# A mixture-of-experts kernel: later slot weights, a weight place used once, and a hint ahead of a jump

## The reference, cut to what matters

```python
def hier_moe(h, w_group, b_group, w_expert, b_expert, w1, w3, w2):
    gl = (hf @ w_group) + b_group                 # 4 groups: the best one by argmax
    g_w = softmax(gl)[g_idx]
    el = (hf @ w_expert)[group g_idx] + b_expert  # 8 experts in it: the best two
    vals, idx = top_k(softmax(el), 2)
    weights = g_w * vals / sum(vals)
    # each of 32 experts works on the rows routed to it:
    y = (silu(x @ w1[e]) * (x @ w3[e])) @ w2[e]   # 1024 -> 512 -> 1024, float32
    # and its rows, times their weights, are added to their tokens
```

## Time and profile before

| | |
|---|---|
| median of 3 runs | 1852.88 us |
| profiled execution | 1853.75 us, span 1851.7 us |
| TensorE busy | 1764.1 us, 95% |
| VectorE / ScalarE / GpSimd busy | 48% / 33% / 7% |
| DMA | 333.57 MB, 180 GB/s over the span |
| mean granted TensorE clock | 0.984 of full |

### The profile page before, as it was taken

The page is one execution under the profiler, slowest core; times in us unless marked ns, Lnnn a source line. Parts: engine busy times, 40 slices in busy tenths (PEclk is TensorE's granted clock), DMA queues, the critical chain, the costliest instruction groups (busy, mean ns, idle before and its releaser), DMA issues.

```text
span 1851.7 us, 25714 instructions
## 1 busy us (share of the span) xinstructions
PE 1764.1 (95%) x10733; PEld 1333.8 (72%) x10733; DVE 893.7 (48%) x1841; ACT 619.6 (33%) x1080; POOL 136.8 (7%) x96
## 2 busy tenths in 40 slices
PE   6999999997999999999989999998999899999998
PEld 5878766886655555555569967666788798888886
DVE  4355454454355555645553577655734532222223
ACT  3434454422111111111242456554524432222222
POOL 1000110221000000000001000011101000000221
PEclk9999999998999999999999999998999999999999
DMA  6512100358899999999955221013420232223201
GB/s 251 191 46 81 57 23 24 131 195 332 330 406 416 402 401 399 400 416 413 429 214 186 91 106 67 1 46 123 162 92 12 91 103 91 93 90 137 91 23 46
DMA packets 76449, 333.57 MB, mean 180 GB/s; under 512 B 6407, under 2 KB 14215, under 8 KB 63400
## 3 DMA queue, kind: packets, MB, share of 16 engines
q1 hardware_dynamic: 72472, 325.04, 45.4%
q0 software_dynamic: 2560, 4.20, 0.7%
q10 hardware_dynamic: 1296, 2.62, 0.4%
HBM read 325.55 MB, written 10.49 MB: 181 GB/s over the span
## 4 chain that ended last, share of the span: by engine, by line
PE 82%; DMA 7%; DVE 5%; ACT 3%; issue 2%; POOL 0%; SPq 0%; DVEq 0%; ACTq 0%; POOLq 0%
PE ps L558 78%; DMA arenaf<-in_w 2%; DMA splitf<-in_w 2%; DMA hf<-in_w 2%; PE ps L977 1%; PE ps L2975 1%; PE ps L2113 1%; DVE arenaf L3057 1%; PE ps L812 1%; DVE splitr L623 0%; ACT splitr L634 0%; DVE arenaf L3075 0%; ACT arenaf L966 0%; DVE hr L866 0%; DVE xf L3353 0%
## 5 line engine op out<-in xcount | busy, mean ns | idle before, releaser
L558 PE MATMUL ps<-hr,splitr 128*128 128x512 f32 (+1 forms) x2784 | 576.2, 367 | 6.7 <-POOL hr L909 4.3
L558 PEld LDWEIGHTS ps<-hr,splitr 128*128 128x128 f32 x2784 | 474.9, 192 | 87.7 <-issue 4.9
L558 PE MATMUL ps<-splitr,hr 128*128 128x512 f32 (+1 forms) x1488 | 273.8, 344 | 2.2 <-DVE hr L1074 1.4
L558 PEld LDWEIGHTS ps<-splitr,hr 128*128 128x128 f32 x1488 | 234.3, 190 | 35.8 <-issue 2.0
L623 DVE TENSOR_TENSOR splitr<-ring,splitr 128x2048 fp32r<-128x2048 f32 x61 | 142.8, 2343 | 230.6 <-ACT splitr L634 230.5
L2233 DVE TENSOR_TENSOR xf<-xf,ps 128x512 f32<-128x512 f32 x248 | 153.5, 682 | 70.8 <-PE ps L558 70.6
L634 ACT CAST splitr<-ring 128x2048 fp32r<-128x2048 f32 x61 | 116.1, 1905 | 143.9 <-PE ps L558 142.8
L2187 ACT ACTIVATE junkr<-ps,arenaf 64x512 fp32r<-64x512 f32 x62 | 42.3, 682 | 296.6 <-PE ps L558 295.9
L623 DVE TENSOR_TENSOR splitr<-arenaf,splitr 128x2048 fp32r<-128x2048 f32 x27 | 63.3, 2345 | 104.9 <-ACT splitr L634 104.9
L558 PE MATMUL ps<-arenaf 128*64 128x128 f32 (+7 forms) x784 | 103.1, 342 | 5.5 <-ACT arenaf L984 3.5
L558 PE MATMUL ps<-splitr,otr 128*128 128x512 f32 x384 | 88.6, 391 | 1.2 <-DVE arenaf L3828 1.2
(11 more groups left out here) (408 smaller groups left out, 1983.0 us busy)
## 6 DMA issues: line engine op xcount, KB each, us to landing
ring<-in_w SPq DMA_DIRECT2D x22, 2048.0 KB, 31.6
arenaf<-in_w SPq DMA_DIRECT2D x22, 2048.0 KB, 31.6
splitf<-in_w SPq DMA_DIRECT2D x21, 2048.0 KB, 34.7
hf<-in_w SPq DMA_DIRECT2D x20, 2048.0 KB, 32.0
ring<-in_w_in SPq DMA_DIRECT2D x11, 2048.0 KB, 12.0
otf<-in_w SPq DMA_DIRECT2D x11, 2048.0 KB, 32.0
ring<-in_w_gate_up SPq DMA_DIRECT2D x7, 2048.0 KB, 7.8
arenaf<-in_w_in SPq DMA_DIRECT2D x4, 2048.0 KB, 8.8
```

The lines of the kernel that those rows point to most:

```text
L558: return te.matmul(out, lhsT, rhs, start=start, stop=stop)
```

## The change

Four things are changed.

1. The products that make the slot weights leave `pe_router` and become `pe_slot_weights`, called for expert 0 behind both up products and the second expert's first transposes. VectorE's two steps behind them move in the same way (`ve_slot_weights`).
2. A tenth place is added (`carve(7168, KC)`, in the arena where the router's tables lie). It holds one entry only, the 26th (w3 of expert 3): no entry follows it there. All later entries move to other places, and the first three loads behind the experts are tied to uses one entry later. SyncE loads it in `sp_router`, when the first gather, the slot roots and OW8 are done.
3. To make room, the tables that are still read then (O8, rk8, tokens, cnt) move to the arena's end, and B8, OW8 and R8 into `junk`. The overflow tables, computed in the same room, wait for the tenth place to be used, so VectorE's pieces begin at expert 4, with two pieces at experts 4 and 5.
4. TensorE's branch past the overflow code is written out as `br_cond` with a `BRANCH_PREFETCH_HINT` that stands ahead of the down product of expert 29.

```diff
         SLOT = [ring0[:, 0:KC], ring0[:, KC:2 * KC], arena[:, 0:KC], OT[:, 0:KC], Hf[:, KC:2 * KC],
-                Sf[:, 0:KC], Sf[:, KC:2 * KC], Hf[:, 0:KC], carve(3072, KC)]
+                Sf[:, 0:KC], Sf[:, KC:2 * KC], Hf[:, 0:KC], carve(3072, KC), carve(7168, KC)]
...
-        extra_places = (3, 8, 5 + wo_end[0] % 2, 7, 5 + wo_end[1] % 2, 4)
+        once = 9
+        extra_places = (3, 8, 5 + wo_end[0] % 2, 7, 5 + wo_end[1] % 2, 4, once)
...
-            if n < len(entries) and not (n >= moe_end and experts_alone):
+            if n < len(entries) and place[c] != once and not (n >= moe_end and experts_alone):
...
-        O8, e8, rk8, q8 = v3(32, 8), v3(1, 8), v3(1, 8), v3(32, 8)
+        O8, rk8 = thirds(carve(11312, 256), 8), thirds(carve(11864, 8), 8)
+        e8, q8 = v3(1, 8), v3(32, 8)
...
-        B8, OW8 = thirds(carve_r(10800, 256), 8), thirds(carve(11056, 256), 8)
+        B8, OW8 = thirds(junk_r[:, 0:256], 8), thirds(junk[:, 256:512], 8)
...
+            def pe_slot_weights():
                 ps = take("slot weights")
...
                 vstep(ve.tensor_tensor(OW8, O8, W8.broadcast_to([128, 8, 32]), ALU.mult), ("slot weights",))
+            def ve_slot_weights():
                 for w in ve_at(("weight sum",)):
...
                 sp_load(more_first + 5)
+                for w in sp_at(("rows", 0), ("root sum",), ("slot weights",)):
+                    sp.wait_ge(*w)
+                sp_load(more_first + 6)
...
                     if b == 0:
                         pe_first_rows(1)
+                        pe_slot_weights()
                     if b < 31 and b % 2:
                         pe_rows((b + 1) // 2)
+                    if b == 30 and live:
+                        branch_ahead.append(te.mark_branch_hint_location())
                     if b:
                         pe_down(b - 1)
...
-                    if 2 <= b < 22:
-                        go(places_, 1)
+                    if 4 <= b < 22:
+                        go(places_, 2 if b < 6 else 1)
...
             def ve_extra_places():
+                for w in ve_at(("entry used", more_first + 6)):
+                    ve.wait_ge(*w)
...
-                extra(te, pe_at, body)
+                if not live:
+                    return extra(te, pe_at, body)
+                te.br_cond(extra_count(te, pe_at) > 0, "overflow", "no_overflow").branch_hint(branch_ahead[0])
+                with nc.body("overflow", valid_engines=[te.engine]):
+                    extra_bodies(te, pe_at, body)
+                    te.br("no_overflow")
+                nc.switch_bb("no_overflow")
```

More of the change, by code:

```diff
@@ L427, in build @@
         upper_r, ones_r = rtr(128)[1], rtr(128)[1]
-        tokens = rt(8).rearrange("p (t o) -> p t o", o=1)
-        Ck, cnt = Ck5[:, 0:4, :], Ck5[:, 4, :]
-        B8, OW8 = thirds(carve_r(10800, 256), 8), thirds(carve(11056, 256), 8)
+        tokens = carve(11824, 8).rearrange("p (t o) -> p t o", o=1)
+        Ck, cnt = Ck5[:, 0:4, :], carve(11832, 32)
+        B8, OW8 = thirds(junk_r[:, 0:256], 8), thirds(junk[:, 256:512], 8)
         R8_, R8r_ = rtr(8 * CAP)
-        R8r, R8 = thirds(R8r_, 8), thirds(R8r_.bitcast(F32), 8)
+        X8r, X8 = thirds(R8r_, 8), thirds(R8r_.bitcast(F32), 8)
+        R8r, R8 = thirds(junk_r[:, 512:1024], 8), thirds(junk_r[:, 512:1024].bitcast(F32), 8)
         rsc, wsc, idf = (carve(11680 + 32 * i, 32) for i in range(3))
@@ L440, in build @@
         xs8, bb8, tb8, t8, rr8 = (v3(1, 8) for _ in range(5))
-        OX = thirds(carve(11552, 8 * NXC), 8)
-        BX = thirds(carve_r(11312, 8 * NXC), 8)
+        OX = thirds(carve(11056, 8 * NXC), 8)
+        BX = thirds(carve_r(10800, 8 * NXC), 8)
         assert R[0] <= 10800, R[0]
@@ L2234, in ve_sum @@
                     *ve_done("x summed", ("xsum", b, half, t), ("free", "xc", b, half, t)))
+            branch_ahead = []
             def pe_experts():
@@ L2259, in pe_experts @@
                         for n in range(8):
-                            mm(ps[0:CAP, 0:NXC], R8r[:, n, :], BX[:, n, :], n == 0, n == 7)
+                            mm(ps[0:CAP, 0:NXC], X8r[:, n, :], BX[:, n, :], n == 0, n == 7)
                         ps = take("extra roots")
                         for n in range(8):
-                            it = mm(ps[0:CAP, 0:2 * NXC], R8[:, n, :], q8[:, n, :], n == 0, n == 7)
+                            it = mm(ps[0:CAP, 0:2 * NXC], X8[:, n, :], q8[:, n, :], n == 0, n == 7)
                         it.then_inc(*pe_done("ranks", ("extra sum",)))
@@ L2328, in ve_experts @@
                         ve_first_rows(1)
+                        ve_slot_weights()
                     if b < 31 and b % 2:
@@ L2412, in ve_extra_places @@
                 vstep(ve.tensor_scalar(bb8, bb8, -1.0, None, ALU.add))
-                for w in ve_at(("idx sum",)):
-                    ve.wait_ge(*w)
-                vstep(ve.tensor_tensor(R8r, row_of(iota, CAP, 8), rr8.broadcast_to([128, 8, CAP]), ALU.is_equal))
+                vstep(ve.tensor_tensor(X8r, row_of(iota, CAP, 8), rr8.broadcast_to([128, 8, CAP]), ALU.is_equal))
                 vstep(ve.tensor_tensor(OX, row_of(iota, NXC, 8), bb8.broadcast_to([128, 8, NXC]), ALU.is_equal))
@@ L2430, in program, with extra_bodies, extra_count, extra @@
             XW = [kview(8, 512)(XSLOT[0]), kview(8, 512)(XSLOT[1]), kview(4, 1024)(XSLOT[2])]
-            def extra(eng, at, body):
+            def extra_bodies(eng, at, body):
+                seen = dict(S.passed)
+                for w in at(*S.ends("experts")):
+                    eng.wait_ge(*w)
+                for j in range(NEX):
+                    body(32 + j)
+                for w in at(*[("end", f"x {j}", e) for j in (NEX - 1,) for e in ("pe", "ve", "se", "ge")]):
+                    eng.wait_ge(*w)
+                S.passed = seen
+            def extra_count(eng, at):
                 for w in at(("extra idx",)):
                     eng.wait_ge(*w)
-                n = eng.value_load(eidu[0:1, NEX:NEX + 1], min_val=0, max_val=NEX)
-                seen = dict(S.passed)
-                with eng.If(n > 0):
-                    for w in at(*S.ends("experts")):
-                        eng.wait_ge(*w)
-                    for j in range(NEX):
-                        body(32 + j)
-                    for w in at(*[("end", f"x {j}", e) for j in (NEX - 1,) for e in ("pe", "ve", "se", "ge")]):
-                        eng.wait_ge(*w)
-                S.passed = seen
+                return eng.value_load(eidu[0:1, NEX:NEX + 1], min_val=0, max_val=NEX)
+            def extra(eng, at, body):
+                with eng.If(extra_count(eng, at) > 0):
+                    extra_bodies(eng, at, body)
             xturn, xheld = [0], {}
```

## The result

Measured beside the kernel before on the same chip, the changed kernel takes 1841.42 us (median of 4 runs, 1838.42 to 1845.1) against 1854.20 (4 runs): ratio 0.9935, 95% interval 0.9918 to 0.9953, thus 12.0 us less (8.7 to 15.2). A second comparison with 10 runs gave 1844.8 us and 0.9950 (0.9933 to 0.9967). Over both, the mean is 1843.2 us (14 runs); the kernel before has a mean of 1854.3 over the 71 runs of the later comparisons: 11.2 us less, plus or minus 1.9. The forecast was 13.9 us less. The profiled execution took 1845.1 us (forecast 1839.8), 8.7 less than the profiled one before, and was the slowest of the four; the second profile of the changed kernel took 1844.4.

A forecast was written before the change was run, and what follows sets the result against it. TensorE, busy 95%, bounds the kernel, losing time to late weights and a stalled branch. Stream 6.6 + hint 7.3 = 13.9 us off the median 1852.88 gives 1839.0 us; own range 1835 to 1843, wider range 1834 to 1849.

The forecast's parts named there:

- marker of the first steps: After the router: added load issued near 458.7, first up product 460.0 to 466.5; later, branch under 0.5 us, keys at full clock.
- The second rival: Expert stage: the weight stream's advance is lost again, 0 to 1 us of 6.6 left, about 1845.6 us; chance 0.10.
- The third: Between hint and jump: the hinted target displaces TensorE's own code, a 6.06 us stop, slower at 1855.2 us; chance 0.05.
- The first rival: At TensorE's jump: the target is still fetched when the branch is taken, only 6.6 us gained, 1846.3 us; chance 0.17.
- the hint, 7.3 us forecast: At TensorE's branch past the overflow code: idle and half clock behind it go, 7.3 us less.
- the 2.9 us for the clock: At the memory keys behind the jump: time lost to TensorE's half clock, expected to be saved, 2.9 us.
- the idle time's 4.42: Behind the branch, ahead of the memory keys: TensorE's idle that no other engine ends, 4.42 us.
- nothing to be given back: Behind the memory keys: TensorE is near its bound to the end and later loads follow its uses, so no gain is lost.
- the stream, 6.6 us forecast: Expert stage: weight loads run earlier by 5.1 + 1.5 = 6.6 us, between 5.8 and 8.9.
- The tenth place: Gap behind the router: one more weight transfer fits wholly inside, everything behind it in the stream is 5.1 us earlier.
- The order: Slot weights behind the up products: first up product ends at 466.5 instead of 468.0, 1.5 us, bounds 0.7 to 4.4.
- some 2 us of idle: Last third of the expert stage, after 744 us: TensorE's idle falls to about 2 us from 8.9.

The follow-up runs named there:

- no_hint: The changed kernel without the hint instruction, TensorE's branch still written out; median 1846.83 us, ratio 0.9956 to the kernel before.
- hint_alone: The kernel before with only the written-out branch and its prefetch hint added; median 1851.04 us, ratio 0.9978 to the kernel before.
- short_jump: The kernel before with TensorE's overflow code replaced by one idle instruction, without a hint; median 1850.92 us, ratio 0.9984 to the kernel before.
- place_alone: The changed kernel with the slot weights back in the router, tenth place and hint kept; median 1845.37 us, ratio 0.9947 to the kernel before.
- order_alone: The changed kernel without the tenth place, later slot weights and hint kept; median 1844.32 us, ratio 0.9937 to the kernel before.

## Why the prediction was right, and where it was not

**Right: sign, range, and the places.** The waits for weights and the stall at the jump were the two things to be had. Every marker of the first steps came within 0.2 us (issue 458.6, product 460.0 to 466.3, branch under 0.5 us, keys at the full clock), and nothing behind the stage changed. The second rival (the advance is lost, 0 to 1 us left) is refuted by no_hint (7.0 ± 2.0 us). The third (the hint displaces TensorE's own code) is refuted: in hint_alone the only idle times of TensorE between hint and jump are 0.83, 0.59 and 0.32 us, which the kernel before has too, and it is faster than before. The first rival (the hint has no effect) is refuted by the branch in hint_alone (0.41 us) beside no_hint (6.10), and with it, for this chip, the sentence of the Trainium skill in "Runtime: NRT & Kernel Launch", section "Instruction fetch mechanics", that prefetch is purely sequential: a branch that took 6.06 us takes 0.41 behind a hint. The other half of what the Trainium skill says there stands: without a hint a far branch costs 5.2 to 6.1 us in four profiles, and 0.24 when its target is near.

**Mis-sized: the hint, 7.3 us forecast, 2.8 to 4.6 measured.** In profiles the step is as forecast (7.4 us), but that first profile was the dearest of the five in which the branch stalled (four without a hint, one with the late hint): the idle was 4.42, 4.01, 4.42, 4.12 and 3.46 us, and the keys took 3.01, 2.73, 2.67, 2.42 and 1.61 us above 13.97, together 6.6 on the mean. The four timed comparisons give 2.8 ± 1.4 (hint_alone, 4.0 ± 1.7 by its own comparison), 3.2 ± 1.7 (short_jump), 4.2 ± 2.5 (with and without the hint in the changed kernel) and 4.6 ± 2.3 us (with the stream ahead): about the idle time alone. The failed term is the 2.9 us for the clock, and the idle time's 4.42 was at the top of its spread. The clock term fails in a second way: 5.93 us at half clock should have raised the mean granted clock of a whole run by 5.93/2/1852 = 0.0016. Against 71 runs before it changed by -0.0003 ± 0.0010 (hint_alone) and -0.0001 ± 0.0011 (short_jump); with and without the hint in the changed kernel it is 0.0006 ± 0.0016 higher, which decides nothing. So in the two kernels with the hint or the short jump alone the half-clock time saved at the keys doesn't show up over the run. In the profiles one sees where such time can go: hint_alone, short_jump and the changed kernel's first profile all have a slow product (6.4 to 6.5 us) behind the 2.6 us wait, the first profile before has not. Whether one causes the other, or both are chance, is open; "I expect nothing to be given back" was too sure in either case.

**Right in size, in part by luck: the stream, 6.6 us forecast, 7.0 ± 2.0 measured.** The tenth place was to give one transfer of 5.1 us because it ran wholly in the gap. It does so in place_alone, but takes 9.6 to 10.3 us from issue to landing: for the time in the gap I had used what a transfer takes off a full stream, though rows 6 showed 8.2 us from issue to landing for a transfer right behind the router, with no gathers beside it. In the changed kernel it sticks out of the gap by 2.6 and 3.8 us. The order was to give 1.5 us; with the clock's return at chance it gave 1.7 and 3.1 in the two profiles, and 3.5 in order_alone, all inside the bounds 0.7 to 4.4. That the larger gain of one and the overlap of the two about cancel was not foreseen, and ± 2.0 us leaves room for both to be off.

**Missed: what is left of the waits.** I expected some 2 us of idle behind 744 us; it is 4.2 and 4.4. Aligned, the landings in the changed kernel's two profiles are ahead of the first profile before by 6.7 and 6.8 us at the fifth of these loads, as forecast, by 6.0 and 6.1 at the 12th, 5.2 and 5.3 at the 38th, 4.0 and 5.2 at the 61st, and 4.7 and 5.9 at the 81st. So 1 to 2 us of the lead are lost little by little over the stage. In no_hint, whose stream of weights is the same, the lead is 7.0 us at the fifth and 7.2 at the 80th and the idle time 2.6 us, near the forecast. The loss is thus not fixed by the order of the loads; no experiment looked for its cause.

**Missed: a later start.** The prediction put nothing on what stands ahead of the router, where no instruction is changed. In the two pairs of profiles the router starts 1.8 and 3.8 us later in the changed kernel, which is 1.8 of the 5.2 us and 3.8 of the 5.3 us by which the two profiled executions fall short of the forecast gain (they gain 8.7 and 8.6 us). If the executions without the profiler have it too, it is part of the shortfall in time as well; no run tests that (more in the last section).

## What to carry to other kernels

A gap in the stream of transfers can be filled by an extra buffer or closed by earlier work; price the two together, and for the room in the gap take the time from issue to landing (8 to 10 us here), not a transfer's share of the full stream (5.1). A stall that one profile shows at one place has a spread of its own: price the idle time, and count the half clock behind it as a bonus that may not come. The cost of a long jump of TensorE went with a hint 31.6 us ahead and with a near target; 7.0 us ahead was too late in the one profile that shows it. A stage measured in two profiles of one kernel differed by 2.4 us, so small parts of a change want timed runs or several profiles.

## What the runs showed of the hardware

- The granted clock around TensorE's waits is not fixed by the program. The first up product behind the router took 3.67 us with the waits filled, else 4.80 to 5.08 in seven profiles and 6.17 to 6.45 in the six others; the product behind the 2.6 us wait took 3.67 (2 profiles), 5.36 (5) and 6.42 to 6.50. The same program gave different values on two executions.
- A branch hint is obeyed by TensorE: the far branch took 0.40 to 0.41 us in the eight profiles with a hint 31.5 to 31.6 us ahead, 5.77 with one 7.0 us ahead, and 5.16 to 6.10 in four without.
- These falls explain much of the spread of single runs. In a fit over 159 runs with one level for each kernel, 0.001 of mean granted clock goes with 1.24 us, and the clock takes up 70% of the spread around the levels. At equal clock the two samples of the changed kernel come out at -9.2 and -9.1 us, the kernel before against itself at -0.1.
- The start of the router varies between 448.2 and 453.4 us though nothing ahead of it is changed. The six profiles of the changed kernel's full code with a hint have 452.0 to 453.4, the eight others 448.2 to 450.9. In order of the start, the mean granted clock up to 446 us, by the traces' records of it, is 0.992 in the four earliest (448.2 to 449.4), 0.989 in the two profiles before (449.5 and 450.2), and 0.981 or 0.985 in the rest (450.7 to 453.4). So the later start goes with more time at half clock ahead of it. Why the six latest are all of one code, which differs from the others only behind that point, I did not find.
